# Two blocks in one launch: rotary tables and vector rows moved into the MLP and tail chains, and the second block's layers written out without a loop

## What is computed

```python
def second_block(x, p, positions, ln_mix, w_in, gdn_conv, ...):
    h = x
    for i in range(DEPTH):
        hn = rmsnorm(h, ln_mix[i])
        (g_q, ..., s_v) = jnp.split(hn @ w_in[i], SPLIT_POINTS, axis=-1)
        o_gdn = gated_deltanet(...)
        o_nsa = native_sparse_attention(..., positions, ...)
        o_sb = stick_breaking_attention(s_q, s_k, s_v)
        mix = jnp.concatenate([o_gdn, head_rmsnorm(o_nsa, ...), head_rmsnorm(o_sb, ...)], axis=-1)
        h = h + mix @ w_out[i]
        h = h + conv_ffn(rmsnorm(h, ln_ffn[i]), w_up[i], ffn_conv[i], w_down[i])
        gate = jax.nn.sigmoid(rmsnorm(h, ln_ple[i]) @ w_ple_gate[i])
        h = h + gate * rmsnorm(p[i] @ w_ple[i], ple_norm[i])
    return rmsnorm(h, ln_final)
```

## Time and profile before

| | |
|---|---|
| median of 3 runs | 4045.7 us (4043.0 to 4049.84) |
| profiled execution | 4044.3 us, span 4042.5 us |
| instructions | 47341 |
| PE busy | 3630.1 us (90%) |
| DVE busy | 1795.8 us (44%) |
| ACT busy | 1312.2 us (32%) |
| POOL busy | 424.4 us (10%) |
| granted PE clock, mean | 0.924 |
| DMA, mean | 79 GB/s |

### The profile page before, as it was taken

How to read it: one execution, slowest core, us unless ns; L and a number is a source line. 1 busy time by engine, 2 the same in 40 slices (tenths; PEclk the granted TensorE clock), 3 DMA queues, 4 the chain that set the end, 5 groups by cost and what they waited for, 6 DMA issues and landing times. The chain is left out here.

```text
span 4042.5 us, 47341 instructions
## 1 busy us (share of the span) xinstructions
PE 3630.1 (90%) x19533; PEld 2782.0 (69%) x19533; DVE 1795.8 (44%) x2767; ACT 1312.2 (32%) x2028; POOL 424.4 (10%) x347
## 2 busy tenths in 40 slices
PE   5989889999997899977897879999889978799998
PEld 4777656888785678865666437788666754477886
DVE  4775556433324343324442434454454424345434
ACT  3332453222323332323222433333342224333333
POOL 0002001210001012000230000310002300003100
PEclk7999999999998899998996969999999969699999
DMA  6641324422220222213100012323031000123230
GB/s 228 204 146 37 87 73 151 169 94 80 84 72 16 104 82 75 107 44 106 48 16 23 1 47 68 110 77 122 23 113 38 12 22 1 68 73 104 74 120 26
DMA packets 230550, 317.82 MB, mean 79 GB/s; under 512 B 13101, under 2 KB 169622, under 8 KB 228926
## 3 DMA queue, kind: packets, MB, share of 16 engines
q1 hardware_dynamic: 230334, 314.77, 23.4%
HBM read 312.09 MB, written 6.85 MB: 79 GB/s over the span
## 5 line engine op out<-in xcount | busy, mean ns | idle before, releaser
L497 PE MATMUL out<-h_lo,w_hi 128*128 128x512 f32 x2608 | 1043.6, 400 | 42.1 <-DVE w_lo L488 37.8
L488 DVE TENSOR_TENSOR w_lo<-ring,w_hi 128x1024 fp32r<-128x1024 f32 (+2 forms) x473 | 581.3, 1235 | 996.9 <-ACT w_hi L483 992.0
L498 PE MATMUL out<-h_hi,w_hi 128*128 128x512 f32 x2608 | 1022.5, 392 | 0.0
L499 PE MATMUL out<-h_hi,w_lo 128*128 128x512 f32 x2608 | 1022.1, 392 | 0.0
L483 ACT ACTIVATE w_hi<-ring 128x1024 fp32r<-128x1024 f32 (+2 forms) x473 | 483.3, 1028 | 1173.2 <-PE out L499 1080.1
L497 PEld LDWEIGHTS out<-h_lo,w_hi 128*128 128x128 f32 x2608 | 494.2, 189 | 166.3 <-issue 50.1
L498 PEld LDWEIGHTS out<-h_hi,w_hi 128*128 128x128 f32 x2608 | 494.2, 189 | 112.9 <-issue 11.0
L499 PEld LDWEIGHTS out<-h_hi,w_lo 128*128 128x128 f32 x2608 | 493.8, 189 | 103.7
L497 PE MATMUL item_banks<-h_lo,w_hi 128*128 128x512 f32 (+1 forms) x696 | 316.7, 455 | 14.2 <-DVE w_lo L488 5.1
L498 PE MATMUL item_banks<-h_hi,w_hi 128*128 128x512 f32 (+1 forms) x696 | 279.2, 401 | 0.0
L499 PE MATMUL item_banks<-h_hi,w_lo 128*128 128x512 f32 (+1 forms) x696 | 279.0, 401 | 0.0
(11 more groups left out here) (487 smaller groups left out, 4641.2 us busy)
## 6 DMA issues: line engine op xcount, KB each, us to landing
ring<-in_mlp_w SPq DMA_DIRECT2D x30, 2048.0 KB, 7.9
ring<-in_w_up SPq DMA_DIRECT2D x44, 1024.0 KB, 6.5
tiles<-in_mod_w SPq DMA_DIRECT2D x80, 512.0 KB, 4.6
ring<-in_e_w_in SPq DMA_DIRECT2D x48, 512.0 KB, 4.2
ring<-in_w_in SPq DMA_DIRECT2D x22, 1024.0 KB, 5.2
ring<-in_w_down SPq DMA_DIRECT2D x10, 2048.0 KB, 7.7
ring<-in_o_w_in SPq DMA_DIRECT2D x7, 2048.0 KB, 8.0
tiles<-in_mod_w SPq DMA_DIRECT2D x8, 1024.0 KB, 8.6
```

The costliest lines, as they stand in the source:

```text
L488: return nc.vector.tensor_tensor(lo.bitcast(F32R), x, hi, ALU.subtract)
L497: nc.tensor.matmul(out, wh, xl, start=start, stop=False, **kw)
L498: nc.tensor.matmul(out, wh, xh, start=False, stop=False, **kw)
L499: return nc.tensor.matmul(out, wl, xh, start=False, stop=stop, **kw)
```

## The change

`rotary_tables` becomes `rotary_tables_lane` in `odd_tail`'s region, with planned times from the beginning of the fourth `ups` block. The tile for the table is now called `turned_table`. The steps are the same, spread 4 us apart; PE waits for the store 150 us after the begin. The constants `inv_freq` and `half_sign` move to the first constants, from which three unused ones are dropped, so the load of `const2` in that stage goes.

`layer_vectors` is split. `fetch_vectors_lane` issues the 16 DMAs, spaced by 2 us of planned time: for layer 0 in `odd_tail` from the third `downs` block, for layer 1 in the first layer's tail from the second `downs` block. PE waits for them 120 us later. `turn_vectors_lane` is in the mixer's region at planned time 0: three transposes into one PSUM bank, one DVE copy of 243 columns. `vec_rows` is now held for the whole program. The loop is a Python loop, so both layers are written out and addresses are constants.

```diff
-    with (
-        k.sbuf("vec_rows", [P, 3, P]) as vec_rows, k.psum("turned", [P, 3, S]) as turned,
-        stage(nc, "rows_in vec_turned") as (block, rows_in, vec_turned),
-    ):
...
+def fetch_vectors_lane(k, r, lane, a, l, BEGIN):
+
+    nc = k.nc
+    rows = vector_rows(a, l)
+    rows_in, = r.semaphores("next_vectors", "rows_in")
+
+    @lane.sync
+    def _(sp):
+        for n, (g, at, count, col, width, src) in enumerate(rows):
+            yield BEGIN + 2.0 * n
+            sp.dma_start(k.vec_rows[at:at + count, g, col:col + width], src).then_inc(rows_in, 16)
+
+    @lane.tensor
+    def _(pe):
+        yield BEGIN + 120.0
+        pe.wait_ge(rows_in, 16 * len(rows))
+
+
+def turn_vectors_lane(k, r, lane, bank):
+
+    nc = k.nc
     used = (V_FCONV, 88, 44)
...
+    vec_turned, vec_out = r.semaphores("vectors", "vec_turned vec_out")
+
+    @lane.tensor
+    def _(pe):
+        at = 0
+        for g in range(3):
+            n = used[g]
+            last = nc.tensor.transpose(bank[:, at:at + n], k.vec_rows[0:n, g, :], k.at["ident"][0:n, 0:n])
+            at += n
+        last.then_inc(vec_turned, 1)
+        yield 0.0
+
+    @lane.vector
+    def _(dve):
+        dve.wait_ge(vec_turned, 1)
+        nc.vector.tensor_copy(k.vec2[:, 0:sum(used)], bank[:, 0:sum(used)]).then_inc(vec_out, 1)
+        dve.wait_ge(vec_out, 1)
+        yield 0.0
+
+    @lane.scalar
+    def _(act):
+        yield 10.0
+        act.wait_ge(vec_out, 1)
+
+
+def rotary_tables_lane(k, r, lane, a, BEGIN):
...
+    @lane.sync
+    def _(sp):
+        yield BEGIN - 20.0
+        sp.dma_start(pos_int, a["positions_2"][0].partition_broadcast(P)).then_inc(pos_in, 16)
+        yield BEGIN + 90.0
+        sp.wait_ge(cos_done, 1)
+        sp.wait_ge(signed, 1)
+        sp.dma_start(k.turn_rows, table[:, :, :]).then_inc(kept, 16)
+
+    @lane.tensor
+    def _(pe):
+        yield BEGIN + 150.0
+        pe.wait_ge(kept, 16)
+
+    @lane.vector
+    def _(dve):
+        yield BEGIN
+        dve.wait_ge(pos_in, 16)
+        nc.vector.tensor_copy(ang, pos_int).then_inc(step, 1)
+        yield BEGIN + 4.0
+        dve.wait_ge(step, 1)
+        nc.vector.tensor_scalar(ang, ang, k.at["inv_freq"], None, ALU.mult).then_inc(step, 1)
...
+        yield BEGIN + 44.0
+        nc.vector.tensor_scalar(ang, ang, edge, -edge, ALU.min, ALU.max).then_inc(step, 1)
+        yield BEGIN + 70.0
+        dve.wait_ge(sin_done, 1)
+        nc.vector.tensor_scalar(table[:, 1, :], table[:, 1, :], k.at["half_sign"], None, ALU.mult).then_inc(signed, 1)
+
+    @lane.scalar
+    def _(act):
+        yield BEGIN + 52.0
+        act.wait_ge(step, 12)
+        nc.scalar.activation(table[:, 1, :], ang, ACT.Sin).then_inc(sin_done, 1)
+        nc.scalar.activation(table[:, 0, :], turns, ACT.Sin).then_inc(cos_done, 1)
+        nc.scalar.preload_act_table_set(EXP_LN_SET)
...
@@ odd_tail
+        rotary_tables_lane(k, r, r.lane(0.0, 1.0), a, ups[3].begin)
+        fetch_vectors_lane(k, r, r.lane(0.0, 1.0), a, 0, downs[2].begin)
@@ second_mixer
+            turn_vectors_lane(k, r, r.lane(0.0, 1.0), stat_banks[:, 1, :])
@@ layer_tail
+        if l == 0:
+            fetch_vectors_lane(k, r, r.lane(0.0, 1.0), a, 1, downs[1].begin)
...
@@ second_blocks
-        rotary_tables(k, a)
-        with k.nc.Fori(0, 2) as l:
-            layer_vectors(k, a, l)
+        for l in range(2):
             second_mixer(k, a, l, tiles, lambda f: k.vec2[:, V_MIX + f:V_MIX + f + 1])
             layer_tail(k, a, l, tiles)
```

More of the change, by code:

```diff
@@ new lines, in rotary_tables_lane @@
+    ang, turns, over = (r.sbuf(name, [P, S])[:, :] for name in ("ang", "turns", "over"))
+    pos_int = r.stack.enter_context(k.sbuf("pos_int", [P, S], I32))[:, :]
+    table = r.sbuf("turned_table", [P, 2, S])
+    (pos_in, step, sin_done, cos_done, signed, kept) = r.semaphores("angles", "pos_in step sin_done cos_done signed kept")
+    @lane.sync
[6 more added lines that the diff above has]
+        sp.dma_start(k.turn_rows, table[:, :, :]).then_inc(kept, 16)
@@ new lines, in _ @@
+    @lane.tensor
[10 more added lines that the diff above has]
+        nc.vector.tensor_scalar(ang, ang, k.at["inv_freq"], None, ALU.mult).then_inc(step, 1)
+        yield BEGIN + 8.0
+        dve.wait_ge(step, 2)
+        nc.vector.tensor_scalar(turns, ang, 1.0 / turn, magic, ALU.mult, ALU.add).then_inc(step, 1)
+        yield BEGIN + 12.0
+        dve.wait_ge(step, 3)
+        nc.vector.tensor_scalar(turns, turns, -magic, None, ALU.add).then_inc(step, 1)
+        for n, c in enumerate((c1, c2, c3)):
+            yield BEGIN + 16.0 + 4.0 * n
+            dve.wait_ge(step, 4 + n)
+            nc.vector.scalar_tensor_tensor(ang, turns, -c, ang, ALU.mult, ALU.add).then_inc(step, 1)
+        yield BEGIN + 28.0
+        dve.wait_ge(step, 7)
+        nc.vector.tensor_scalar(turns, ang, np.pi / 2, None, ALU.add).then_inc(step, 1)
+        yield BEGIN + 32.0
+        dve.wait_ge(step, 8)
+        nc.vector.tensor_scalar(over, turns, edge, -turn, ALU.is_gt, ALU.mult).then_inc(step, 1)
+        yield BEGIN + 36.0
+        dve.wait_ge(step, 9)
+        nc.vector.tensor_tensor(turns, turns, over, ALU.add).then_inc(step, 1)
+        yield BEGIN + 40.0
+        dve.wait_ge(step, 10)
+        nc.vector.tensor_scalar(turns, turns, edge, -edge, ALU.min, ALU.max).then_inc(step, 1)
+        yield BEGIN + 44.0
[3 more added lines that the diff above has]
+        nc.vector.tensor_scalar(table[:, 1, :], table[:, 1, :], k.at["half_sign"], None, ALU.mult).then_inc(signed, 1)
```

78 lines of the change are left out of this document (6 added, 72 removed).

## The result

| | before | after |
|---|---|---|
| median, same chip | 4045.7 us | 4020.5 us |
| all executions | 4037.7 to 4049.8 | 4015.4 to 4027.8 |
| profiled execution (span) | 4044.3 (4042.5) | 4020.5 (4018.7) |
| instructions | 47341 | 46953 |
| PE busy | 3630.1 us | 3640.0 us |

The ratio is 0.9941, with an interval from 0.9925 to 0.9957. Two more measurements of the changed kernel, on other chips, gave 0.9955 [0.9940, 0.9969] and 0.9945 [0.9926, 0.9963]. So the change gains 18 to 24 us. It was forecast at 4006 us, in a range from 4000 to 4013.5: the sign was right, the size was not.

A forecast was written before the change was run, and what follows sets the result against it. PE, the busy engine, bounds the kernel, so savings come only where it stands still: 28.5 + 10.4 + 0.4 + 0.6 = 39.9 us off 4044.3 gives 4004.4, with 1.4 for the median 4005.8, said as 4006; range 4000 to 4013.5.

The forecast's parts named there:

- First boundary: From the first block's end to the second's first layer: both stages go, 29.42 us shrink to 0.95, saving 28.5 us.
- second: Between the two layers: rows fetched beside the first layer's tail, loop's jump gone, 11.32 us shrink to 0.95, saving 10.4.
- loop's end: From DVE's last addition to the last norm's first square: without counter and compare, 1.35 us become 0.95, saving 0.4.
- The 0.95 us for a passage: Time left at each boundary for passing from one region into the next, taken from two rows, 0.91 and 0.96.
- Turning the rows: Three transposes and one copy at a mixer's start, done during ACT's first squares: cost nothing, bound 0.6 us for both layers.
- The rotary tables in the MLP: DVE's 13 instructions and ACT's table loads and sines in the third mixer's MLP: cost 0, upper bound 10.3 us.
- The rival by which part is given back there: Sines, table loads or DVE's steps hold up PE in the MLP: 3.7 to 10.3 us, put at 4010; chance 0.12.
- SP's queue: Positions, table store and twice 16 short fetches added to SP's DMA issues, covered by its waits: cost 0.
- Addresses: Moves and register operations ahead of DMA issues inside the loop go: 0.6 us gained, at most 2.2, at least nothing.
- The rival on the clock: At the second boundary the shorter pause may keep PE's clock up: at most 4 us more gained, 4002; chance 0.05.
- its terms upwards (0.6, 0.6 and 3): What could lengthen the forecast time: 0.6 us for addresses, 0.6 for turning the rows, some 3 for scatter between runs.

The follow-up runs named there:

- the long kernels: Kernels with all 19533 matmuls written out in the program, among them the changed kernel, 4020.5 us.
- the short ones: Kernels with 13606 matmuls in the program, by a run-time loop or one layer left out, among them the kernel before, 4045.7 us.
- those with the later sums: Second half of the modulation's sums taken one MLP block later, in the changed kernel (4013.3 us) and in it with the loop kept (4013.9 us).

## Why the prediction was wrong

- **First boundary, 28.5 us; second, 10.4; loop's end, 0.4.** The first two are right, 28.33 and 10.26; the third was 0.10, small either way. The 0.95 us for a passage was 1.06 to 1.25. That part of this was the loop itself is borne out: with the loop kept the second boundary is 3.7 us (4.0 in its first trace), not 1.06.
- **Turning the rows, 0.** Right: PE 0.83 us, DVE 0.41, under the squares. The split of the first weights comes 8.66 us after the first square, 8.54 before.
- **The rotary tables in the MLP, 0.** Right, and by its reason: no wait was added, and from the split at 1501.1 us to the last root of the MLP at 1797.2 all 20 traces have 296.1 us. The rival by which part is given back there is wrong. The Trainium skill's page ScalarE: Activation LUTs, section What ACT_TABLE_LOAD costs, has 2.66 us for a switch with its drain; the trace shows 1.28 us for a load and no drain between it and the sine.
- **SP's queue, 0.** Right: the store was issued at 1600.3 us, 22 us after the signed sine, between two loads of blocks, and PE waited for none of them.
- **Addresses, 0.6 gained.** Wrong, though small. The gain is not seen: the first split is 0.1 us later after the first square. The step counted moves of 29 ns in SP's queue and left out that the program gets longer. With the loop kept, the boundary between the layers is 3.73 us long and without it 1.06: the jump, with what the loop does around it, costs 2.7 us. The Trainium skill's page Runtime: NRT & Kernel Launch, section Instruction fetch mechanics, says that a taken branch can stall the fetch of instructions, when its target is not among the pages at hand, and gives this as one reason why kernels prefer full unrolling. That the jump costs time agrees with the 2.7 us, though no trace shows whether it is the fetch; on the preference the kernel before disagrees, whose ratio was 1.0044 when its loop was written out.
- **What failed** is none of the terms for the moved parts but the silent premise of the sum, that whatever the change does not touch keeps its time ("all of it moves up"); what a longer program and a shifted clock cost was put at nothing without a reason. Two things break it. First, the program's length: the `ups` loads from `mlp_w` land 0.7 us later, at the modulation's sums PE waits 2.7 to 4.1 us instead of 0 to 1, and the clock there is 0.85 instead of 0.90 or 0.95. From 790 to 1049 us the long kernels take 262.0 to 263.7 us and the short ones 256.6 to 259.3, those with the later sums left out, **4.7 us** by the means. Second, half clock in other places of the same instructions: the first layer came out **7.2 us** longer, the second 3.5 by the means of two and three traces. Sum: 38.7 - 4.7 - 7.2 - 3.5 = 23.3 us, against 18 to 24 measured. These are measured lengths, so that the sum comes out shows where the time went. Of its reasons only part of the first is shown by an experiment, the sums' place; why this kernel's layers have more half clock stays open.
- **The rival on the clock** looked for a change in the right quantity, in the wrong place and with one sign. At the second boundary the clock did fall less (0.76 over the 7 us from 2902, 0.54 in the earlier trace rows), and it gave nothing: PE's sums took 8.83 us as against 8.76 and the root still stood behind the weights' split. The Trainium skill's page TensorE: Matmul & The Clock Gate, section What's actually happening, says that activity lifts the clock; the traces agree within a stretch (the 340 us of uninterrupted work have 1.00), but the kernel as a whole got no more clock for having fewer pauses: 0.924 and 0.925.
- **The range** was too narrow for this reason. It took 3 us up and 1 down for scatter, where its own three runs lie 4.1 us above and 2.7 below their median; and its terms upwards (0.6, 0.6 and 3) give 4010, not 4009.5. Neither slip would have reached 4020. The pattern of half clock differs between kernels with the same instructions by up to 16 us in one layer, and nothing in one profile of one kernel shows that.

What stays open: why these loads are slower in a longer program (their size, their queue and the number of packets of instruction fetch in the whole run, 157 and 155, are alike, and the same shape from another tensor is not slower), and what decides a kernel's pattern of half clock. Whether it is the length of the pause ahead of the first layer was not tried by itself: with 11, 21 and 39 us of it the first layer took 1083.1, 1085.7 and 1085.2 us, which shows no order.

## What to carry to other kernels

A pause of up to 40 us that is taken away is worth about its length, but in a long kernel in which PE waits now and then for 1 to 4 us, an edit can also shift the places at which its clock falls; put ten microseconds of that into the range, and profile both kernels twice before you explain a difference of that size. When a sum of parts does not come out, look for stretches with the same instructions and compare length and granted clock: where the clock is 1.00 they agree to hundredths. Writing a loop out is not free even if it removes jumps and register work: compare the landing times of loads that the edit does not touch, tensor by tensor and shape by shape, since a median over all can hide that only some are late. Give a load that is issued behind a large one more lead than it needs today; here it was worth 5.5 us in one kernel and 3.7 in the other.

## What the hardware showed that I had not expected

- A program with 19533 matmuls in its code instead of 13606 had the 2 MB `ups` loads of one tensor land 0.7 us later (8.7 to 8.8 us instead of 7.9 to 8.1), in a part of the program that was the same, while loads of the same size and shape from another tensor kept their 8 us.
- The same two waits of PE can cost different amounts of clock: of two pieces with the same 56 matmuls and 5.6 and 6.2 us of waits, one took 20.2 us at a clock of 0.92 and one 23.5 at 0.78. And the clock fell to 0.90 over 35 us in which PE was busy throughout.
- With the same instructions, a layer took 1070.3 us in one kernel and 1086.6 in another, each repeated to within 0.2 us.
